# Two transformer blocks with 32 experts on one core: slots and constants moved by 128 bytes, router logits taken from the ungained sum, the first weight unit loaded in halves, a store issued from another engine, the convolution's last steps spread over more heads

## The reference, cut to what matters

```python
def conformer_conv(u, w_dw, b_dw, ln_g, ln_b):
    a, gt = jnp.split(u, 2, axis=-1)
    h = a * jax.nn.sigmoid(gt)
    h = causal_depthwise_conv(h, w_dw, b_dw)      # 31 taps, 512 channels
    h = layernorm(h, ln_g, ln_b)
    return jax.nn.silu(h)
...
    x = x + cross_attention(...)                   # ends with o @ w_co
    x = x + moe_ffn(rms_norm(x, ffn_norm_g), w_router, b_router, w_gu, b_gu, w_down, b_down)
    return rms_norm(x, final_norm_g)
...
def moe_ffn(h, ...):
    logits = xt @ w_router + b_router              # 32 experts
    top_val, top_idx = lax.top_k(logits, 4)
    gates = jax.nn.softmax(top_val)
    # each expert: clamped_swiglu(xb @ w_gu[e] + b_gu[e]) @ w_down[e] + b_down[e]
```

## Time and profile before

| what | us |
|---|---|
| median of three runs | 1724.79 |
| the profiled execution | 1726.6 |
| its span, first to last instruction | 1724.8 |
| PE busy in it | 1578.4 (92%) |
| DVE busy | 753.1 (44%) |
| ACT busy | 482.6 (28%) |
| POOL busy | 182.2 (11%) |
| mean granted clock of PE | 0.99 |
| a 1 MB `w_in` unit, issue to landing, median of 36 | 5.3 |

### The profile page before, as it was taken

How to read it: one execution, slowest core, us unless ns; L and a number is a source line. 1 busy time by engine, 2 the same in 40 slices (tenths; PEclk the granted TensorE clock), 3 DMA queues, 4 the chain that set the end, 5 groups by cost and what they waited for, 6 DMA issues and landing times.

```text
span 1724.8 us, 22680 instructions
## 1 busy us (share of the span) xinstructions
PE 1578.4 (92%) x9684; PEld 998.8 (58%) x9684; DVE 753.1 (44%) x1333; ACT 482.6 (28%) x825; POOL 182.2 (11%) x208
## 2 busy tenths in 40 slices
PE   7999999999999999989999988888898888889886
PEld 6998899999999989973333322223232322323221
DVE  6798777979884788551221211111121212111121
ACT  4245666455553564530110101010010101001001
POOL 0201102515530041020000000000000000000000
PEclk9999999999999999999999999999999999999999
DMA  9866455556655635658999999999999999999996
GB/s 219 173 206 167 120 135 175 165 171 192 178 194 174 197 117 189 247 199 331 422 421 422 421 421 421 420 421 421 421 421 421 421 422 422 420 421 421 422 421 270
DMA packets 195002, 527.89 MB, mean 306 GB/s; under 512 B 18546, under 2 KB 136351, under 8 KB 145743
## 3 DMA queue, kind: packets, MB, share of 16 engines
q1 hardware_dynamic: 191008, 519.23, 78.8%
q0 software_dynamic: 3344, 6.93, 2.6%
q10 hardware_dynamic: 542, 0.21, 0.1%
HBM read 524.70 MB, written 1.62 MB: 305 GB/s over the span
## 4 chain that ended last, share of the span: by engine, by line
DMA 45%; PE 44%; DVE 7%; ACT 2%; issue 1%; SPq 0%; ACTq 0%; DVEq 0%
PE bank L604 43%; DMA slot_ring<-in_w_down 15%; DMA slot_late<-in_w_down 8%; DMA slot_high<-in_w_down 8%; DMA slot_memx<-in_w_down 8%; DVE slot_ring_r L1972 2%; DMA slot_ring<-in_w_gu 2%; DMA slot_memt<-in_w_gu 2%; DMA slot_ring<-in_w_in 2%; ACT high_r L1535 1%; DVE h_sb L1980 1%; DVE conv L1980 0%; DVE rstd L2014 0%; DVE stat L2190 0%; DVE stat L2408 0%
## 5 line engine op out<-in xcount | busy, mean ns | idle before, releaser
L604 PE MATMUL bank<-h_hi_r,high_r 128*128 128x256 f32 x1000 | 286.7, 287 | 7.7 <-DVE slot_ring_r L1972 3.4
L1972 DVE TENSOR_TENSOR slot_ring_r<-slot_ring,high_r 128x1024 fp32r<-128x1024 f32 x198 | 250.3, 1306 | 78.1 <-ACT high_r L1535 75.8
L604 PE MATMUL bank<-h_lo_r,high_r 128*128 128x256 f32 x1000 | 283.1, 283 | 0.0
L1976 DVE TENSOR_SCALAR ga<-bank 128x512 f32<-128x512 f32 x32 | 22.1, 691 | 591.1 <-PE bank L604 591.1
L604 PE MATMUL bank<-h_hi_r,slot_ring_r 128*128 128x256 f32 x952 | 269.5, 283 | 0.0
L1535 ACT ACTIVATE high_r<-slot_ring 128x1024 fp32r<-128x1024 f32 x198 | 198.0, 1051 | 64.2 <-PE bank L604 43.4
L604 PEld LDWEIGHTS bank<-h_hi_r,high_r 128*128 128x128 f32 x1000 | 191.3, 191 | 11.3 <-DVE h_lo_r L1972 4.3
L1535 ACT ACTIVATE th_e<-ga 128x512 f32<-128x512 f32 x32 | 20.2, 630 | 624.0 <-DVE ga L1976 624.0
L604 PEld LDWEIGHTS bank<-h_lo_r,high_r 128*128 128x128 f32 x1000 | 191.4, 191 | 0.1
L604 PEld LDWEIGHTS bank<-h_hi_r,slot_ring_r 128*128 128x128 f32 x952 | 182.2, 191 | 0.0
L604 PE MATMUL bank<-slot_ring,xg 128*64 128x512 f32 x528 | 124.6, 603 | 11.4 <-DMA slot_ring<-in_w_gu 11.4
(11 more groups left out here) (441 smaller groups left out, 2901.0 us busy)
## 6 DMA issues: line engine op xcount, KB each, us to landing
slot_ring<-in_w_gu SPq DMA_DIRECT2D x66, 1024.0 KB, 27.0
slot_high<-in_w_gu SPq DMA_DIRECT2D x50, 1024.0 KB, 26.7
slot_ring<-in_w_down SPq DMA_DIRECT2D x49, 1024.0 KB, 26.6
slot_last<-in_w_gu SPq DMA_DIRECT2D x38, 1024.0 KB, 27.1
slot_ring<-in_w_in SPq DMA_DIRECT2D x36, 1024.0 KB, 5.3
slot_late<-in_w_gu SPq DMA_DIRECT2D x32, 1024.0 KB, 26.7
slot_high<-in_w_down SPq DMA_DIRECT2D x25, 1024.0 KB, 27.0
slot_ring<-in_w_up SPq DMA_DIRECT2D x44, 512.0 KB, 4.8
```

Of the source, the lines that this page charges most:

```text
L604: return e.matmul(o, lhs, rhs, start=start, stop=stop, skip_group_check=True)
L1972: return e.tensor_tensor(o, i, j, op)
L1976: return e.tensor_scalar(o, i, s1, None, op1)
```

## The change

What it does:

- **Slots and constants**: everything in SBUF from `COLS` on lies 32 columns (128 bytes) further, down to the ring and high slots; the slots counted from the end keep their place. The constants' array gets 96 unused columns.
- **First unit**: `ub` 0 is loaded in four pieces of 256 KB, rows 0 to 511 of both column groups first, on a semaphore of their own; ACT begins on the first half at once. ACT splits `ub` 1 before `load_rows(1)`.
- **Store**: ACT issues the two stores to `diag_dram`, behind `qa` 1; POOL has nothing in front of `lams`, `wrt`, `brt` and `pos_i` any more.
- **Convolution**: taps 13 and 14 in head 0, tap 15 in head 1, steps 16 in head 2, 18 and 19 in head 3, 20, 21, 22 in heads 4, 5, 6.
- **Residual**: DVE calls `ahead((w, 3))` once behind the last addition, in all three places, in place of `ahead((w, 2))` and `ahead((w, 3))` behind their own.
- **Logits**: the gain is multiplied into `wrt` once, early. The router's products read x, not h, for blocks 0 to 3 before the last `co` product and for 4 to 7 behind it. The squares are summed to one column per token. The norm's factor is applied per token: to the logits, and where h is copied out of PSUM. ACT writes h = x * gain as the sums come in, so that h is turned without a norm.

```diff
+    parts["unused"] = np.zeros((P, -(sum(a.shape[1] for a in parts.values()) - 3) % P))
...
-        CONST, COLS = 0, -(-n_const // 8) * 8 + 64
+        CONST, COLS = 0, -(-n_const // 8) * 8 + 96
...
+        sq_last = tiles(at("sq_last", AR + TT * D, KT * S), KT)
...
+        def two_columns_halved(name, w, c0, c1):
+            unit(name, [(lambda s, j=j, r=r: s.rearrange("p (k n) -> p k n", k=KT)[:, 4 * r:4 * r + 4, j * P:(j + 1) * P],
+                         w[r * 512:(r + 1) * 512, c:c + P].rearrange("(k p) n -> p k n", p=P))
+                        for r in range(2) for j, c in enumerate((c0, c1))])
...
@@ tensor_program, heads of the first attention
-                conv_norm(13 + 3 * n)
...
-                conv_norm(14 + 3 * n)
+                if n in (1, 2):
+                    conv_norm(15 + n)
...
-                conv_norm(15 + 3 * n)
...
@@ tensor_program, from co to the experts
-            add_residual("co", mix_s, lambda k: dve["co split", k // 2], "ffn_g")
...
-            for k in range(KT):
-                q.wait_ge(*dve["h", "ffn_g", k])
-                m = matmul(b[k % 4 * NE:(k % 4 + 1) * NE, 0:S], wrt[:, k, :], h[:, k, :], k < 4, k >= 4)
...
+            def logits(ks):
+                q.wait_ge(*dve["router gains"])
+                for k in ks:
+                    q.wait_ge(*dve["residual", "co", k // 2])
+                    m = matmul(bank("router")[k % 4 * NE:(k % 4 + 1) * NE, 0:S], wrt[:, k, :], x[:, k, :], k < 4, k >= 4)
+                return m
+
+            def token_squares(i):
+                q.wait_ge(*sq_by("ffn_g", i)["square", "ffn_g", i])
+                q.wait_ge(*pool["squares", "ffn_g"])
+                for t in range(TT):
+                    for k in (2 * i, 2 * i + 1):
+                        m = matmul(bank(("ffn_g", "sums"))[:, t:t + 1], sq_last[:, k, t * P:(t + 1) * P], ones[:, 0:1],
+                                   k == 0 and t == 0, k == KT - 1)
+                return m
...
+            for i in range(3):
+                co_unit(i)
+            banks.take(q, "router")
+            logits(range(0, 4))
+            co_unit(3)
+            pe.mark("moe")
+            turn_h(0)
+            banks.take(q, ("ffn_g", "sums"))
+            token_squares(0)
+            logits(range(4, KT)).then_inc(*pe.step("router"))
+            banks.give("router", (dve, "logits"))
+            token_squares(3).then_inc(*pe.step("sums", "ffn_g"))
+            banks.give(("ffn_g", "sums"), (act, ("root", "ffn_g")))
+            q.wait_ge(*act["logit rows"])
+            for t in range(TT):
+                m = matmul(bank("router")[:, S + t * NE:S + (t + 1) * NE], mean_sb[:, t * P:(t + 1) * P], C("stack"), True, True)
+            m.then_inc(*pe.step("logits turned"))
+            turn_h(1)
+            for c in range(2):
                 for t in range(TT):
...
                     turn_back("x_tok", x, t, c, (act, ("x_tok", t, c)))
...
@@ gpsimd_program
-            for i in range(2):
-                q.wait_ge(*dve["diag", i])
-                e.dma_start(diag_dram[i * SWA_H:(i + 1) * SWA_H, :, :],
...
@@ scalar_program
-            q.wait_ge(*landed(("ub", 0)))
+            q.wait_ge(*early_in["early"])
             high(("ub", 0), 0)
...
+            q.wait_ge(*landed(("ub", 0)))
             high(("ub", 0), 1)
...
-            load_rows(1)
...
                 ahead(name)
+                if c == 0:
+                    load_rows(1)
...
+            for i in range(2):
+                q.wait_ge(*dve["diag", i])
+                e.dma_start(diag_dram[i * SWA_H:(i + 1) * SWA_H, :, :],
...
-                conv_norm(13 + 3 * n)
+                if 3 <= n < 7:
+                    conv_norm(16 + n)
...
+                if n == 2:
+                    conv_norm(16)
                 gates(2 * n + 1)
...
+                if n == 2:
+                    conv_norm(18)
...
+                    if norm == "ffn_g":
+                        q.wait_ge(*dve["residual", w, i])
+                        for k in (2 * i, 2 * i + 1):
+                            af(h[:, k, :], x[:, k, :], ACT.Copy, scale=col("ffn_g", k)).then_inc(*act.step("gained", k))
...
+            evac(("logit rows",), mean_sb, bank("router")[:, 0:S], ("router",))
+            q.wait_ge(*pe["sums", "ffn_g"])
+            af(token_norm, bank(("ffn_g", "sums"))[:, 0:TT], ACT.Sqrt, bias=eps_col[EPS2]).then_inc(*act.step("root", "ffn_g"))
...
@@ vector_program
+                for s in {1: (15,), 2: (16,), 3: (18,)}.get(n, ()):
+                    conv_step(s)
                 ahead(("gz", 2 * n))
-                conv_step(13 + 3 * n)
+                for s in {0: (13,), 3: (19,), 4: (20,), 5: (21,), 6: (22,)}.get(n, ()):
+                    conv_step(s)
                 ahead(("gz", 2 * n + 1))
-                conv_step(14 + 3 * n)
+                if n == 0:
+                    conv_step(14)
...
-                    if i >= 2:
-                        ahead((w, i))
+                ahead((w, 3))
...
+                    tt(wrt, wrt, gains.broadcast_to([P, KT, NE]), ALU.mult).then_inc(*dve.step("router gains"))
...
-            apply("ffn_g", x, h)
...
+            for t in range(TT):
+                stt(logit[:, t, :], bank("router")[:, S + t * NE:S + (t + 1) * NE], token_norm[:, t:t + 1], brt, ALU.mult,
+                    ALU.add).then_inc(*dve.step("logits"))
...
+                    stt(ht_lo[:, t, part], bank(("h_tok", t, c))[:, :], token_norm[:, t:t + 1], ht_hi[:, t, part], ALU.mult,
+                        ALU.subtract).then_inc(*dve.step("h_tok lo", t, c))
```

More of the change, by code:

```diff
@@ L558, in after_all, with squares_of @@
                 q.wait_ge(*d[point])
+        def squares_of(norm):
+            return sq_last if norm == "ffn_g" else h
         FOX, SWA, MOBA = "fox", "swa", "moba"
@@ L1043, in tensor_program, with co_unit @@
             pe.mark("ffn start")
-            add_residual("co", mix_s, lambda k: dve["co split", k // 2], "ffn_g")
-            pe.mark("moe")
-            banks.take(q, "router")
-            b = bank("router")
-            q.wait_ge(*wrt_in["wrt"])
-            for k in range(KT):
-                q.wait_ge(*dve["h", "ffn_g", k])
-                m = matmul(b[k % 4 * NE:(k % 4 + 1) * NE, 0:S], wrt[:, k, :], h[:, k, :], k < 4, k >= 4)
-            m.then_inc(*pe.step("router"))
-            banks.give("router", (dve, "logits"))
+            def co_unit(i):
+                project(("co", i), mix_s, lambda k: dve["co split", k // 2], (dve, ("residual", "co", i)))
+            def logits(ks):
[12 more added lines that the diff above has]
+                return m
             def turn_back(name, src, t, c, *until):
@@ L1062, in turn_back, with turn_h @@
                 banks.give((name, t, c), *until)
+            def turn_h(c):
+                for t in range(TT):
+                    q.wait_ge(*act["gained", 4 * c + 3])
+                    turn_back("h_tok", h, t, c, (act, ("h_tok hi", t, c)), (dve, ("h_tok lo", t, c)))
+            for i in range(3):
[16 more added lines that the diff above has]
+            turn_h(1)
             for c in range(2):
                 for t in range(TT):
-                    turn_back("h_tok", h, t, c, (act, ("h_tok hi", t, c)), (dve, ("h_tok lo", t, c)))
-                    if c == 0 and t == 0:
-                        q.wait_ge(*act["logit rows"])
-                        for s in range(TT):
-                            m = matmul(b[:, S + s * NE:S + (s + 1) * NE], mean_sb[:, s * P:(s + 1) * P], C("stack"), True, True)
-                        m.then_inc(*pe.step("logits turned"))
-            for t in range(TT):
-                for c in range(2):
                     turn_back("x_tok", x, t, c, (act, ("x_tok", t, c)))
@@ L1295, in load @@
                 slot_of[name] = slot
-                for view, src in transfers:
-                    e.dma_start(view(slot_f[slot]), src).then_inc(*slot_in[slot].step("unit", name))
+                for i, (view, src) in enumerate(transfers):
+                    if name == ("ub", 0) and i < 2:
+                        e.dma_start(view(slot_f[slot]), src).then_inc(*early_in.step("early"))
+                    else:
+                        e.dma_start(view(slot_f[slot]), src).then_inc(*slot_in[slot].step("unit", name))
                 idle.append((slot, (used_by, name if isinstance(name, tuple) else (name,))))
@@ L2506, in vector_program @@
             least = spread(top8[:, :, TOPK - 1:TOPK])
+            q.wait_ge(*act["root", "ffn_g"])
+            e.reciprocal(token_norm, token_norm).then_inc(*dve.step("token factors"))
             q.wait_ge(*pe["logits turned"])
             q.wait_ge(*brt_in["brt"])
-            tt(logit, bank("router")[:, S:S + TT * NE].rearrange("p (t n) -> p t n", t=TT),
-               brt.rearrange("p (o n) -> p o n", o=1).broadcast_to([P, TT, NE]), ALU.add).then_inc(*dve.step("logits"))
+            own()
+            for t in range(TT):
```

(2 more changed lines are left out.)

39 lines of the change are left out of this document (19 added, 20 removed).

## The result

The changed kernel takes 1699.63 us (four runs, 1698.74 to 1701.13) beside 1725.48 for the kernel before on the same chip: a ratio of 0.9846 with a 95% interval of 0.9827 to 0.9864. The forecast was 1711, with a range of 1705 to 1718. The direction was right. The gain, 25.9 us, is nearly double the forecast's, and the time lies under the range.

A forecast was written before the change was run, and what follows sets the result against it. Transfers were taken to bound the kernel from about 805 us, PE before, so an earlier last release brings the end forward. Terms of 1.7 + 2.0 + 5.5 + 0.6 + 2.9 + 1.0 = 13.7 us gave 1711 us, range 1705 to 1718.

The forecast's parts named there:

- start: Loads and splits of `ub` 0 and 1: earlier first product and no PE idle before `ub` 1, gain 1.7 us (0 to 3).
- store, gap at 86 us: Diagonals' store from ACT, small loads gone from behind it: PE's 2.1 us stall goes, gain 2.0 us (-2 to 2.1).
- first attention: Heads 0 to 7, convolution steps moved: head 3's stall goes, head 4's turns end earlier, gain 5.5 us (3.5 to 7).
- `ahead`, out / out2: DVE's split behind the last addition: 0.8 us lost behind `out`, 1.4 gained behind `out2`, 0.6 in all (-0.5 to 2).
- `co` to pick: Last `co` product to first pick, at +12.15 in place of +16.4, less 1.3 for earlier router blocks: gain 2.9 us (1.5 to 3.6).
- clock behind the pick: PE's half clock from 790 to 797 us may fall once, twice or not: gain 1.0 us (-1.7 to 3.4).
- slots and constants: Places of slots and constants, for the experts' transfers: nothing taken, 2.9 us (0.3% of 954) possible either way.
- The new wait: Before the pick, PE's third and fourth turn of x wait for banks that DVE's `h_tok_lo` frees, until +8.9 us.
- hold back the weights: Rival: ACT's queue serves the store worse, so the stall at 86 us stays or grows: 1713 to 1715 us, chance 0.15.
- DVE takes nothing back: Rival: slower DVE heads or clock falls cut the first attention's gain to 2 to 3 us: 1714 us, chance 0.13.
- the release came forward with the pick: Rival: something thought hidden holds the release at 802.49 us, only what lies before 735 us counts: 1715 us, chance 0.07.
- the stream got faster: Rival claimed the opposite: new offsets slow the expert stream, deciding under 416 GB/s; chance 0.07 together with another loss.

The follow-up runs named there:

- e11: The changed kernel with the first unit, `ub` 0, loaded whole in two transfers under one wait, as before: 1702.24 us.
- e12: The changed kernel with POOL's four small loads held until the second diagonal is made, the store staying on ACT: 1696.83 us.
- e10: The changed kernel with the store of the diagonals back on POOL, in front of the four small loads: 1700.81 us.
- e9: The changed kernel with the convolution's last steps back in their places of before on PE, ACT and DVE: 1707.92 us.
- e13: The changed kernel with DVE's split of the next units behind additions 2 and 3 again, in all three sums: 1699.92 us.
- e14: The changed kernel with the whole router part as before: 1704.21 us.
- e1: The kernel before with the shift of the ring, high and `h_hi` slots alone (COLS 64 to 96): 1713.71 us.
- e8: The kernel before with everything from the column constants to the high slots 256 bytes further on: 1725.06 us, one run.
- e17: The kernel before with only the late, last and mem slots 384 bytes nearer to the start, on multiples of 512: 1721.26 us, one run.
- e4: The changed kernel with slots and constants back in their places of before, the program as changed: 1711.46 us.
- e6: The kernel before with x, h, `h_hi`, small tiles, ring and high slots 128 bytes nearer to the start: 1713.66 us, one run.

## Why the prediction came out as it did

| term | forecast | measured | by |
|---|---|---|---|
| start | +1.7 | -0.3 | places; e11, e12 |
| store, gap at 86 us | +2.0 | +2.2 | places; e10 |
| first attention | +5.5 | +8.1 (7.1 on average) | e9 |
| `ahead`, out / out2 | -0.8 / +1.4 | -0.5 / +3.1 (2.2 on average) | e13's trace |
| `co` to pick | +2.9 | +3.5 (4.4 on average) | places; e14 |
| clock behind the pick | +1.0 | -1.6 (-1.2 on average) | places |
| slots and constants | 0 (+-2.9) | +10.9 | e1 to e8, e17 |
| second to third norm | none | +1.5 | not of the change |

**Slots: the step that failed.** "The trace has slots at several offsets and the share is 1.01 for all together; I take nothing." Both halves were wrong. Of the slots only `h_hi` lay off the others' offset to 256 bytes, and none lay on a boundary, so the trace of before had no aligned case to compare with. And a share of 1.01 says that the engines are busy, not how much they move: it is 1.01 at 421 and at 427 GB/s. The bound of 0.3% had no row under it. The 10.9 us are 1.2% of the 922 us from release to end, and without them the same program (e4) takes 1711.46, against 1711 forecast. That nearness is partly luck, since the other terms missed both ways.

**Start: wrong in sign.** The mechanism was named ("in the middle of the loads of `x` and `ub`"), but its price of 1.2 us, taken between nothing and 2, is 4.3 us (first product 19.15 against 14.85 in e12). The small loads have 400 KB, not 0.3 MB, and what is slow in them is `lams`, not the shortest runs. The halves bring 1.1 us (e11) where 1.7 was taken. The skipped wait for `ub` 1 was right: 2.1 us late at the first product are 0.3 at `ub` 1.

**Store: right in size**, and the forecast's likeliest reading, a source limit that is the same for both queues, holds at 50 to 55 GB/s. The forecast gave the gain to the small loads alone, which no longer stand behind the store. The runs show that half of the engines stay free as well: in e12 the small loads are back behind the store and there is no gap.

**First attention: right in mechanism, 2.6 us too small in this trace, 1.6 on average.** The forecast let the lead shrink by some 0.2 us a head from head 4 (DVE 15.6 us, PE 15.4). But DVE's maxima of heads 4 and 5 lie 15.3 us apart in the changed kernel (209.38 and 224.64), and the lead stays: 9.9 at head 4, 10.0 at head 7. And the narrow end of the range assumed a fall of the clock at head 1. In the changed kernel's trace there was none, but in four of the eight with these steps there was, and it cost 1.3 us.

**`ahead` behind out2: too small.** The reciprocal came 2.6 us sooner against the third norm than in e13 (666.93 - 575.44 against 672.06 - 577.97), where 1.2 was forecast, and the fall of the clock behind the sum (0.79 and 0.87 in the two windows from 675 to 685 us before) went with it: none of the eight kernels with the new order has one there, and ten of the eleven others do, e6 being the one without. The sum had left that out.

**Router: right.** The forecast pick was at +12.15 and came at +12.0; the blocks in front of the last `co` product cost 0.9 where 1.3 was taken. The new wait is there, 1.90 us for the banks of the first h tiles. The row puts it down to ACT, but by the program PE waits there for ACT's high part and DVE's `h_tok_lo` of the same tile. The high parts had ended at 746.00 and 746.57, the two `h_tok_lo` ended at 748.61 and 749.26, and PE went on at 748.72 and 749.38: it waited for `h_tok_lo`, as forecast. What this hides is the clock: it fell to 0.50 in this stretch, so the counts took 2.05 us in place of 1.27.

**Clock: within its bounds, at the poor end.** It fell at 750 us, just before the pick, and again at 774, for 6.8 us each.

None of the rivals came true: the store doesn't hold back the weights, DVE takes nothing back, the release came forward with the pick but for the clock, and the stream got faster where only "slower" had been thought through.

## What to carry to other kernels

When a kernel is bound by transfers, work out each destination's first byte and set it on a multiple of 256, which gave 1.4% here; a DMA share of 1.0 doesn't show the loss, the GB/s beside it do. A bound of a term must have a row under it: for a resource that takes 922 of 1725 us, "nothing" is a claim about every percent of it. Small loads that nothing needs yet don't belong beside the first weights: here they cost 4.3 us at the first product, and issued at 55 us they cost PE nothing. And a size read from one pair of traces can be off by a microsecond; every other kernel with the same instructions is one more measurement of it.

## What was not expected of the hardware

With all slots but one on a multiple of 256, 99% of the 8 KB packets take 309 ns; with none, 23 to 31% do and the mean is 313.4. With half of the transfers on one, the rate is 426 GB/s of 427. 512-byte packets pay 3 to 6 ns of 27 for the same. A store of 8 rows holds half of the engines from ACT's queue and nearly all from POOL's, at the same 50 to 55 GB/s. Beside the first weights, packets that read the same 256 bytes for all partitions took 871 ns each where larger ones, some of them with shorter runs, took 172. The stretch between the second and the third norm took 215.6 or 214.2 us in 17 of 19 traces with unchanged code, with the granted clock at 1.00 in both; why stays open.
